# A stream of weight tiles fetched in pairs: 1 MB into four double buffers in place of 512 KB into eight

## The reference, cut to what matters

```python
def first_block(x, c, ...):
    mod = silu(c) @ w_ada + b_ada                 # one row times 2048 x 12288: six parts of 2048
    sh_a, sc_a, gt_a, sh_f, sc_f, gt_f = split(mod, 6)
    h = rmsnorm(x, g_pre_attn) * (1 + sc_a) + sh_a
    qa, ka, va, qb, kb, vb = split(h @ w_in, 6)   # 2048 x 6144
    oa = rmsnorm(dilated_mixture_attention(rope(qa), rope(ka), va), g_out_a)
    ob = rmsnorm(differential_attention(rope(qb), rope(kb), vb, lam), g_subln_b)
    x = x + gt_a * rmsnorm(concat(oa, ob) @ w_out, g_post_attn)
    h = rmsnorm(x, g_pre_ffn) * (1 + sc_f) + sh_f
    f = (silu(h @ w_gate) * (h @ w_up)) @ w_down  # 2048 x 5632, twice, and back
    return x + gt_f * rmsnorm(f, g_post_ffn)

def second_block(x, mem, ...):
    # h @ w_in (2048 x 5008); latent attention and indexed sparse attention; @ w_out
    # cross attention to 256 memory rows (w_k_cross, w_v_cross act on mem alone)
    # square(relu(h @ w_up)) @ w_down, 2048 x 8192 and back; final rmsnorm
```

## Time and profile before

| | |
|---|---|
| median of 3 runs | 2550.05 us (2549.34 to 2553.55) |
| the profiled execution | 2550.17 us |
| its span, first to last instruction | 2548.9 us |
| busy share of the span | PE 95%, PEld 79%, DVE 63%, ACT 46%, POOL 3% |
| chain that ended last | PE 84%, DVE 8%, DMA 3%, ACT 3% |
| read from HBM | 526 MB, 207 GB/s over the span |

### The profile page before, as it was taken

How to read it: one execution, slowest core, us unless ns; L and a number is a source line. 1 busy time by engine, 2 the same in 40 slices (tenths; PEclk the granted TensorE clock), 3 DMA queues, 4 the chain that set the end, 5 groups by cost and what they waited for, 6 DMA issues and landing times.

```text
span 2548.9 us, 28178 instructions
## 1 busy us (share of the span) xinstructions
PE 2418.8 (95%) x11175; PEld 2010.0 (79%) x11175; DVE 1601.9 (63%) x1706; ACT 1180.1 (46%) x1533; POOL 64.3 (3%) x102
## 2 busy tenths in 40 slices
PE   5989999989999999999989999897899999999998
PEld 4777778878888888788868887786788888788886
DVE  7989798778876657555565666444544444455555
ACT  4454555444434444444454445445544444444443
POOL 3000110000000000000000000000000000000000
PEclk8999999989999999999999999998999999999999
DMA  9998786758775666566646554152466666555553
GB/s 347 386 381 292 282 314 232 269 201 296 264 254 173 198 190 189 169 196 192 193 135 198 170 173 148 53 196 83 149 187 184 189 184 189 177 195 193 194 192 115
DMA packets 219636, 530.23 MB, mean 208 GB/s; under 512 B 16570, under 2 KB 19008, under 8 KB 218864
## 3 DMA queue, kind: packets, MB, share of 16 engines
q1 hardware_dynamic: 218560, 526.71, 62.9%
q0 software_dynamic: 640, 0.63, 0.1%
q10 hardware_dynamic: 304, 1.09, 0.1%
HBM read 526.26 MB, written 2.10 MB: 207 GB/s over the span
## 4 chain that ended last, share of the span: by engine, by line
PE 84%; DVE 8%; DMA 3%; ACT 3%; issue 2%; POOL 1%; DVEq 0%; ACTq 0%; POOLq 0%
PE ps L549 26%; PE ps L551 26%; PE ps L550 26%; PE ps L545 2%; DVE ada_acc L1385 1%; DMA raw<-in_w_in 1%; DVE wlo L1371 1%; DVE silu_gate L1753 1%; PE ps L649 1%; PE ps L672 1%; PE ps L617 1%; DVE ada_acc L1398 1%; ACT whi L982 1%; DMA raw<-in_w_v_cross 1%; PE ps L596 1%
## 5 line engine op out<-in xcount | busy, mean ns | idle before, releaser
L982 ACT ACTIVATE whi<-raw 128x1024 fp32r<-128x1024 f32 (+1 forms) x802 | 848.3, 1058 | 1222.8 <-PE ps L551 1139.4
L1371 DVE TENSOR_TENSOR wlo<-raw,whi 128x1024 fp32r<-128x1024 f32 (+1 forms) x802 | 974.7, 1220 | 540.0 <-ACT whi L982 538.6
L549 PE MATMUL ps<-whi,h_hi 128*128 128x512 f32 (+1 forms) x2016 | 797.7, 396 | 14.3 <-DVE h_lo L1446 5.7
L551 PE MATMUL ps<-wlo,h_hi 128*128 128x512 f32 (+1 forms) x2016 | 786.9, 390 | 0.0
L550 PE MATMUL ps<-whi,h_lo 128*128 128x512 f32 (+1 forms) x2016 | 786.5, 390 | 0.0
L549 PEld LDWEIGHTS ps<-whi,h_hi 128*128 128x128 f32 x2016 | 381.1, 189 | 96.5 <-issue 6.6
L551 PEld LDWEIGHTS ps<-wlo,h_hi 128*128 128x128 f32 x2016 | 380.4, 189 | 79.3
L550 PEld LDWEIGHTS ps<-whi,h_lo 128*128 128x128 f32 x2016 | 381.0, 189 | 75.8 <-issue 0.7
L549 PE MATMUL ps<-whi,src_hi 128*128 128x512 f32 x1024 | 401.9, 392 | 9.2 <-DVE src_lo L1464 4.9
L550 PE MATMUL ps<-whi,src_lo 128*128 128x512 f32 x1024 | 400.9, 391 | 0.0
L551 PE MATMUL ps<-wlo,src_hi 128*128 128x512 f32 x1024 | 400.8, 391 | 0.0
(11 more groups left out here) (265 smaller groups left out, 1443.5 us busy)
## 6 DMA issues: line engine op xcount, KB each, us to landing
raw<-in_w_up SPq DMA_DIRECT2D x216, 512.0 KB, 3.7
raw<-in_w_down SPq DMA_DIRECT2D x216, 512.0 KB, 3.7
raw<-in_w_ada SPq DMA_DIRECT2D x192, 512.0 KB, 6.2
raw<-in_w_in SPq DMA_DIRECT2D x168, 512.0 KB, 4.6
raw<-in_w_gate SPq DMA_DIRECT2D x88, 512.0 KB, 3.8
raw<-in_w_out SPq DMA_DIRECT2D x64, 512.0 KB, 4.2
raw<-in_w_k_cross SPq DMA_DIRECT2D x8, 512.0 KB, 9.2
raw<-in_w_v_cross SPq DMA_DIRECT2D x8, 512.0 KB, 8.6
```

What stands on the lines that cost most here:

```text
L549: T.matmul(dst, ah, bh, start=first, stop=False)
L551: return T.matmul(dst, ah, bl, start=False, stop=last)
L982: A.activation(whi[n % SPLIT][:, 0:size], raw[f % RAW][:, 0:size], ACT.Copy).then_inc(*s_hi.next(n))
L1371: V.tensor_tensor(wlo[n % SPLIT][:, 0:size], raw[w_fetch[n] % RAW][:, 0:size], r32(whi[n % SPLIT][:, 0:size]), ALU.subtract).then_inc(*s_l ...
```

## The change

The ring becomes four pairs of buffers, `raw2`, 1 MB each; buffer 2q + k is the half k of pair q, so consumers read the same memory as before. The order of transfers is rewritten in pairs: weight tiles n + 2 and n + 3, then the ada tiles of n and n + 1, two by two, where a pair of ada tiles is fetched at the place of its even member. Where the two tiles lie suitably in HBM, one transfer of 1 MB brings them (`two_tiles`; also ada tiles from 64 on); the first 64 ada tiles and tiles of odd width remain two transfers of 512 KB, started one behind the other. There is one semaphore for each pair of buffers. SP waits, before it fills a pair, until the second of the two tiles in it has been read, and ACT and DVE wait for the whole pair, even for its first half. The programs of PE, ACT, DVE and POOL stay in their order.

```diff
@@
-    raw = [sb(f"raw{r}", "raw", 4 * KB * r, [TILE]) for r in range(RAW)]
+    raw2 = [sb(f"raw{q}", "raw", 8 * KB * q, [2 * TILE]) for q in range(RAW // 2)]
+    raw = [raw2[r // 2][:, (r % 2) * TILE:(r % 2 + 1) * TILE] for r in range(RAW)]
@@
+    fetch_adas(0)
+    fetch_adas(2)
+    fetch_weights(0)
+    fetch_adas(4)
+    for n in range(0, N_END, 2):
         if n + 2 < N_END:
-            fetch_weight(n + 2)
-        for i in ada_at[n]:
-            fetch_ada(i)
+            fetch_weights(n + 2)
+        for i in ada_at[n] + ada_at[n + 1]:
+            if i % 2 == 0:
+                fetch_adas(i)
@@
-            if f >= RAW:
-                was, j = fetches[f - RAW]
+            if q >= RAW // 2:
+                was, j = fetches[2 * q - RAW]
                 if was == "w":
-                    Y.wait_ge(*s_lo.at(j))
+                    Y.wait_ge(*s_lo.at(j + 1))
                 else:
-                    Y.wait_ge(*s_ada.at(j))
+                    Y.wait_ge(*s_ada.at(j + 1))
...
+            if kind == "w" and i in two_tiles:
+                src = two_tiles[i]
+                Y.dma_start(raw2[r][:, :].rearrange("p (k n) -> p k n", k=src.shape[1]), src).then_inc(*s_raw[r].next(q))
@@
                 f = w_fetch[n]
-                A.wait_ge(*s_raw[f % RAW].at(f))
+                A.wait_ge(*s_raw[f // 2 % (RAW // 2)].at(f // 2))
```

More of the change, by code:

```diff
@@ L211, in r32 @@
         return ap.bitcast(F32)
-    weights = []
+    weights, two_tiles = [], {}
     def col_tiles(w, nk, c0, width=BANK):
@@ L219, in col_tiles @@
             rows = w[2 * j * P:(2 * j + 2) * P, c0:c0 + width]
+            if j % 2 == 0 and len(weights) % 2 == 0 and width == BANK and j + 1 < nk // 2:
+                two_tiles[len(weights)] = w[2 * j * P:(2 * j + 4) * P, c0:c0 + width].rearrange("(k p) n -> p k n", p=P)
             weights.append((rows.rearrange("(k p) n -> p k n", p=P), width))
@@ L224, in row_tiles @@
         n0 = len(weights)
+        for kt in range(nk):
+            two_tiles[n0 + 2 * kt] = w[kt * P:(kt + 1) * P, :].rearrange("p (k n) -> p k n", k=4)
         for kt in range(nk):
@@ L244, in build @@
     for half in range(2):
-        for kt in MIX_ORDER:
+        for n, kt in enumerate(MIX_ORDER):
+            if n % 2 == 0:
+                two_tiles[len(weights)] = a["w_out"][0][kt * P:(kt + 2) * P, half * TILE:(half + 1) * TILE].rearrange("(k p) n -> p k n", p=P)
             weights.append((a["w_out"][0][kt * P:(kt + 1) * P, half * TILE:(half + 1) * TILE], 0))
@@ L296, in build, with fetch_weights, fetch_adas @@
     w_fetch, ada_fetch = {}, {}
[L298 to L306, removed]
-        fetch_ada(i)
[L308 to L312, removed]
+    def fetch_weights(n):
+        for k in range(2):
+            w_fetch[n + k] = len(fetches)
+            fetches.append(("w", n + k))
+    def fetch_adas(i):
+        for k in range(2):
+            ada_fetch[i + k] = len(fetches)
+            fetches.append(("ada", i + k))
+    fetch_adas(0)
[3 more added lines that the diff above has]
+    for n in range(0, N_END, 2):
         if n + 2 < N_END:
-            fetch_weight(n + 2)
-        for i in ada_at[n]:
-            fetch_ada(i)
+            fetch_weights(n + 2)
+        for i in ada_at[n] + ada_at[n + 1]:
+            if i % 2 == 0:
+                fetch_adas(i)
     signals = []
@@ L323, in signal @@
         return signals[-1]
-    s_raw = [signal(f"s_raw{r}", 16) for r in range(RAW)]
+    s_raw = [signal(f"s_raw{q}", 16) for q in range(RAW // 2)]
     s_parc, s_park, s_parl, s_par, s_parg, s_mem, s_x, s_gfin, s_out = (signal(n, 16) for n in ("s_par_c", "s_par_k", "s_par_l", "s_par", "s_par_g", "s_mem", "s_x", "s_gfin", "s_out"))
@@ L444, in sync_program @@
         Y.dma_start(vec1[112:128, :], a["g_post_attn"].rearrange("o (k n) -> (o k) n", n=P)).then_inc(*s_par.next())
-        for f, (kind, i) in enumerate(fetches):
-            r = f % RAW
-            if f == 2:
+        for q in range(len(fetches) // 2):
+            kind, i = fetches[2 * q]
+            r = q % (RAW // 2)
+            if q == 1:
                 Y.dma_start(memt[:, :, :], a["mem_2"][0].rearrange("(m p) d -> p m d", p=P)).then_inc(*s_mem.next())
-            if f == 6:
+            if q == 3:
@@ L468, in sync_program @@
-            Y.dma_start(dst, src).then_inc(*s_raw[r].next(f))
+                    Y.wait_ge(*s_ada.at(j + 1))
+            for k in range(2):
+                one_tile = raw[2 * r + k]
+                if kind == "w" and i not in two_tiles:
+                    src, width = weights[i + k]
+                    Y.dma_start(one_tile[:, 0:2 * width].rearrange("p (k n) -> p k n", k=2), src).then_inc(*s_raw[r].next(q))
+                elif kind == "ada" and i < 64:
+                    _, c, kt = ADA[i + k]
+                    src = a["w_ada"][0][kt * P:(kt + 1) * P, 0:2 * D].rearrange("p (t n) -> p t n", t=2)[:, :, c * BANK:(c + 1) * BANK]
+                    Y.dma_start(one_tile.rearrange("p (t n) -> p t n", t=2), src).then_inc(*s_raw[r].next(q))
@@ new lines, in sync_program @@
+            if kind == "w" and i in two_tiles:
+                src = two_tiles[i]
+                Y.dma_start(raw2[r][:, :].rearrange("p (k n) -> p k n", k=src.shape[1]), src).then_inc(*s_raw[r].next(q))
+            elif kind == "ada" and i >= 64:
+                part, kt, _ = ADA[i]
+                src = a["w_ada"][0][kt * P:(kt + 1) * P, part * D:(part + 1) * D].rearrange("p (k n) -> p k n", k=4)
+                Y.dma_start(raw2[r][:, :].rearrange("p (k n) -> p k n", k=4), src).then_inc(*s_raw[r].next(q))
@@ L1376, in ada @@
             f = ada_fetch[i]
-            V.wait_ge(*s_raw[f % RAW].at(f))
+            V.wait_ge(*s_raw[f // 2 % (RAW // 2)].at(f // 2))
             dst = acc[ACC_OF[part]][:, half * TILE:(half + 1) * TILE]
```

13 lines of the change are left out of this document (1 added, 12 removed).

## The result

| | before | after |
|---|---|---|
| median | 2549.7 us (2548.6 to 2553.55, 4 runs) | 2606.92 us (2603.19 to 2609.13, 4 runs) |
| the profiled execution, and its span | 2550.17, 2548.9 us | 2606.44, 2605.1 us |

The change makes the kernel slower by 2.2%: ratio 1.022, with a 95% interval of 1.0202 to 1.0238. The forecast was 2569.2 with a range up to 2590. The direction was right; the size, 57 us in place of 19, was not, and the time lies outside the range.

What follows compares the result with a forecast made beforehand. PE was taken as 84% of the chain, with DMA full in the first three slices and DVE the chain in places. Terms 7.2 + 4.5 + 3.7 + 3.6 = 19.0 us on 2550.17 gave 2569.2 us, range 2552 to 2590.

Steps and rivals of the forecast that it cites:

- the loop of beats 0 to 28: First 145 us: a pair is refilled only after its second `low`; 12 rounds of 8.5 us, +7.2 us.
- the pairs keep up from 145 to 188 us: PE is the chain there; a weight pair is wanted 7 us or more after it is freed, against 5.9: no cost.
- the reciprocals: Gate and up stage: late up tiles delay `low` at four reciprocals with ada tiles around them, +3.6 us.
- the 6.4 us of the upper end: Longest landing assumed for a pair, with halves as slow as in a half-loaded queue; total near 2594 us.
- The start: First beats: ada tiles 4 and 5 land as a pair at 31.8 us, making `low(1)` 1.0 us late.
- t = 28 and t = 68: Ada pairs held over beats without ada tiles delay `low(32)` and `low(72)`: +4.5 and +3.7 us.
- five catch-ups: Places where DVE runs at its fastest pace: nothing in the sum, up to 1 us each for the range.
- three kinds of place: Where the ring can matter: the first 145 us, DVE runs around 200 and 340 us, gate and up reciprocals.
- rival 2: Faster, 2543 us: larger transfers run at 410 GB/s from 24 to 145 us, saving 7.1 us; chance 0.06.
- Absorbed: 2551 to 2555 us: DMA goes on without a bubble and PE's two-tile lag takes up the stalls; chance 0.13.
- faster: 2543 us: larger transfers go faster where DMA is the bound, from 24 to 145 us; chance 0.06.
- Worse, above 2590: Landings under load nearer 6.4 us, and stalls wherever an ada pair lies across beats; chance 0.11.

Runs made afterwards that it cites:

- e1_split: The changed kernel, but with every pair filled by two transfers of 512 KB on the pair's semaphore: 2608.41 us.
- e7_no_straddle: The changed kernel with the ada tile of t = 25 moved, so that ada pairs fall in neighbouring beats around the gaps: 2593.03 us.
- e9_late_pairs: The kernel before, with pairs by one 1 MB transfer only behind the last ada tile (some 735 us on): 2550.55 us, ratio 0.9999.
- e10_pairs_old_order: The kernel before in its own order of transfers, with both readiness and release of buffers in twos: 2551.56 us.
- e8_ring6: The kernel before with six raw buffers in place of eight, nothing else: 2552.6 us.

## Why the prediction was wrong in size, step by step

The steps that failed are three. The landing in the loop of beats 0 to 28 was mis-sized: 4.85 us in the sum, 5.8 measured (+13.9 us over the forecast there). The sum ended that loop at `low(27)` and held that the pairs keep up from 145 to 188 us (+9.0). And the first `w_out`, where the ring is as tight, had no term (+8.2). With 6.3 us at small places, 0.9 behind 730 us and 1.3 less than forecast at the reciprocals that is the difference between 19 and 56. Even the 6.4 us of the upper end would have given 2594: a longer landing alone does not reach the measured time.

**Beats 0 to 28: +7.2 forecast, +21.1 measured at `low(27)`.** The loop was the right one, with the right pieces in the right order (`low` frees the pair, landing, two ada tiles, `low`). The term that was mis-sized is the landing under this load. I took 4.85 us from T, for an unloaded queue. From the end of the second `low` to the start of the ada pair that takes its buffers it is 5.7 us in the round shown above (92.27 to 97.95) and 5.3 to 6.5 in the twelve rounds, a mean of 5.8. The rest of a round, two ada tiles, `low` and now and then other work of DVE, takes 3.8 us, for 3.7. That is 9.6 a round, and from `low(3)` at 42.9 to `low(27)` at 158.0 the 12 rounds took 9.6 each. The formula was sound, and the bound of 6.4 us that I kept for the range gave 10 us a round. The measured landing lies nearer to that bound; I chose the lower value on the ground of a size (the one transfer of 1 MB) and not of a load.

Why the landing is longer, the trace shows in part. In the slices from 92.5 to 98 us 1.5 MB pass, where the pair waited for has 1.05 MB. So the pair doesn't pass alone: some 0.5 MB of what is started behind it pass with it, worth an estimated 1.2 us at 386 GB/s. I had let the pair land as in an empty queue, though the second ada pair, whose buffers are already free, stands right behind it in SP's order and is started at T too. No run took the second pair away, so that this is all of the excess isn't shown. The Trainium skill ("DMA: Bandwidth & Descriptors", Bandwidth and Anatomy of one DMA) would have 2.0 us and the bytes at 436 GB/s, an estimated 4.4 us for 1 MB, by a fit to transfers started by GpSimd, where SP starts these; the page of after has 4.8 for `w_down` and 5.2 for `w_up`, where PE is the bound, and the loop has 5.8. By that estimate the forecast would have been still farther off.

**The start: +1.0 forecast, +1.8 measured.** Ada tile 4 was to start at 31.8. After, against the earlier trace rows:

```profile
32.67 1.28 DVE L1411 SCALAR_TENSOR_TENSOR ada_acc<-raw,silu_c,ada_acc 128x1024 f32<-128x1024 f32 x1 [2.64 <-DMA raw<-in_w_ada]
```

The step held; the landing was again too short, by 0.9 us.

**145 to 188 us: nothing forecast, +9.0 measured** (`low(27)` to `low(37)`). I had ended the loop with `low(27)`. It goes on as long as two ada tiles come with each beat, to beat 28, and the chain above has its last turn at 170.87; `low(30)` is 24.5 us late. The step that failed here is that the pairs keep up from 145 us on. The rest comes behind the loop, while PE catches up. PE's clock has a part that I can't separate. The same 45 us of both kernels, before:

```profile
145.00:190.00 45.00, 43.04 (x199) 35.74 (x200) 38.19 (x38) 22.37 (x26) 0.00 (x0) 0.97 1.02 379
```

After:

```profile
145.00:190.00 45.00, 37.16 (x145) 30.30 (x144) 31.38 (x33) 13.02 (x17) 0.00 (x0) 0.77 0.90 321
```

The granted clock is 0.77 there for 0.97: PE had been busy for 9.9 of the 15 us from 165 to 180, idle for the rest, and in the chain its matmuls then stand 0.43 us apart from 183 to 192.7, the lower level of 1.2 GHz. No run held the clock fixed, so its share of the 9 us stays open. e1_split, in the same order, had 0.85 in these 45 us and was 2.9 us less late at `low(37)`, but 0.8 us later than after by t = 31.

**t = 28 and t = 68: +4.5 and +3.7 forecast, +4.2 and +4.0 measured.** Here the steps were right in place and size. The ada tile of t = 28 and `low(32)` by t, on DVE in after, against the earlier trace rows:

```profile
232.53 1.28 DVE L1398 SCALAR_TENSOR_TENSOR ada_acc<-raw,silu_c,ada_acc 128x1024 f32<-128x1024 f32 x1
...
240.22 1.23 DVE L1384 TENSOR_TENSOR wlo<-raw,whi 128x1024 fp32r<-128x1024 f32 x1 [4.08 <-ACT whi L995]
```

And t = 68, against the earlier trace rows:

```profile
379.26 1.28 DVE L1398 SCALAR_TENSOR_TENSOR ada_acc<-raw,silu_c,ada_acc 128x1024 f32<-128x1024 f32 x1
...
386.81 1.23 DVE L1384 TENSOR_TENSOR wlo<-raw,whi 128x1024 fp32r<-128x1024 f32 x1 [3.94 <-ACT whi L995]
```

The ada tile ends at 233.8 and `low` starts 6.4 us later, for a forecast of 5.9; in the second, 6.3. At t = 28 the queue was empty, and the chain has the landing at 5.27 us: 0.4 more than I took for it even there. e7_no_straddle, which loses nothing at either place, confirms the cause.

**The rest up to 500 us: nothing forecast, some 6.9 at small places, 0.6 given back** (2.3 between `low(37)` and t = 31, 4.6 between t = 32 and t = 71). I had allowed 1 us at each of five catch-ups in the range, but not in the sum.

**The first `w_out`, 500 to 530 us: nothing forecast, +8.2 measured.** This is the step that was missing. I had named three kinds of place where the ring matters, and this stage, in which each beat has an ada tile and the last ones two, wasn't among them. The kernel before shows it, in a stretch that is not among:

```profile
495.00:530.00 35.00, 35.00 (x172) 29.60 (x171) 31.69 (x30) 14.74 (x16) 0.00 (x0) 1.00 0.99 365
```

DMA has a share of 0.99 and DVE 31.7 of 35 us: as tight as the first stage. The two slices of the page in which it lies have 269 and 201 GB/s, means with idle neighbours. In slices of 0.9 us the stretch above reaches 440 GB/s, so the 410 that rival 2 took for the fastest rate of the trace was not the fastest. In after the chain of that stage goes three times through the landing of an ada pair, and two of these landings are longer than any on the chain in the first stage (6.2 us at most):

```profile
541.49 10.32 DMA raw<-in_w_ada
...
556.61 7.33 DMA raw<-in_w_ada
...
567.61 5.00 DMA raw<-in_w_ada
```

No run was made for this stage alone; e7_no_straddle, with its ada tiles paired otherwise, loses 4.2 us in it.

**The reciprocals: +3.6 forecast for four, +2.3 measured from t = 127 to the first, and nothing at the next three.** At the first the mechanism is the one described: ACT waits for up 4, and `low` of up 5 is 1.3 us later than up 3 was.

```profile
640.97 1.06 ACT L995 ACTIVATE whi<-raw 128x1024 fp32r<-128x1024 f32 x1 [3.86 <-DMA raw<-in_w_up]
```

One us more is lost ahead of it, in the gate tiles. At the later three `low` is up to 1.9 us late against the level and catches up before the reciprocal (55.1 to 55.3 us at all four). I had counted each as on the path because of the earlier trace rows; the slack of the tiles ahead took it up.

**Behind 730 us: nothing forecast, +0.9 measured**, and e9_late_pairs, whose ring pairs only there, costs nothing (ratio 0.9999). Right, within what one trace tells.

**The rivals.** "Absorbed" and "faster" are out: the stream runs dry in each round, and larger transfers are worth nothing (e1_split, e9_late_pairs). "Worse, above 2590" is what happened, and in part for the reason that it named, landings near 6.4 us under load (5.8 in the mean, which alone would not have come to 2590); I gave it 0.11. Its second half is right too: pairs across beats cost more places than two. What it lacked was the order: with that of before, e10_pairs_old_order loses 1 us with the same pairs.

## What to carry to other kernels

Before buffers of a ring are joined, write down the order in which they are read: here joined pairs cost nothing that can be told where the old order was kept and the two parts are read one right after the other, and a dry queue in every round where other readers of the same ring stand between them. Reading them side by side is not the whole of it: with new pairs and a reading order made to fit, more than half of the first stage's loss stayed. When a loop goes through a transfer, use the landing under the load that this loop itself makes, with all that is issued at the same moment, and not the landing of a lone transfer; if two rows bound it far apart, the range must treat both ends as likely. And ask for stretches of DMA's share over all of a kernel, in pieces no longer than its shortest stage, before you say where the stream is the bound.

## What the runs showed of the hardware

- With several transfers queued their size made no difference here: 512 KB in rows of 2 KB moved 387 GB/s from 80 to 120 us, and 1 MB in place of 2 x 512 KB changed nothing, in a kernel with tight stages (2608.41 and 2606.92 us, the first a single run) and where PE is the bound (ratio 0.9999). The Trainium skill ("DMA: Bandwidth & Descriptors", Bandwidth) asks for transfers of 1 MB or more and doesn't say how many are under way; with several queued these runs don't bear that out.
- Where PE is the bound, a transfer of 1 MB landed in 4.8 us (`w_down`, rows of 8 KB) and 5.2 (`w_up`, pieces of 2 KB), one of 512 KB in 3.7. In a loop that emptied the queue and then started two pairs at once, the first 1 MB was of use 5.3 to 6.5 us later.
- Six buffers of 512 KB carried 384 GB/s from 80 to 120 us in e8_ring6, against 387 with eight in the kernel before.
